# Block two's recurrence: two streams by halves of the tokens, or four streams by quarters with one PSUM bank each

## The reference, cut to what matters

```python
w_log = -softplus(-(w0 + tanh(wd) @ w_lora_up)) - 0.5
decay = exp(-exp(w_log))
a = sigmoid(a0 + ad @ a_lora_up)
g = sigmoid(gd) @ g_lora_up
kk = k * k_k;  kk = kk / max(norm_per_head(kk), 1e-12)
k = k * (1.0 + (a - 1.0) * k_a)
# per token and head, state is 64 x 64:
sa = einsum('bhvk,bhk->bhv', state, -kk_t)
state = state * w_t + sa (x) (kk_t * a_t) + v_t (x) k_t
y = einsum('bhvk,bhk->bhv', state, r_t)
# then: normalised per head, times ln_x_w, plus ln_x_b, plus (sum(r * k * r_k) * v), times g
```

## Time and profile before

| | |
|---|---|
| median of 3 runs | 3462.05 us |
| lowest and highest run | 3459.52 and 3464.85 us |
| profiled execution, first to last instruction | 3458.7 us |
| TensorE busy | 3282.1 us (95%), 24008 matmul rows |
| VectorE, ScalarE, GpSimd busy | 1732.3, 1221.7, 76.4 us |
| chain that ended last | TensorE 79%, VectorE 12%, ScalarE 6% |

### The profile page before, as it was taken

How to read it: one execution, slowest core, us unless ns; L and a number is a source line. 1 busy time by engine, 2 the same in 40 slices (tenths; PEclk the granted TensorE clock), 3 DMA queues, 4 the chain that set the end, 5 groups by cost and what they waited for, 6 DMA issues and landing times.

```text
span 3458.7 us, 55898 instructions
## 1 busy us (share of the span) xinstructions
PE 3282.1 (95%) x24008; PEld 2729.2 (79%) x24008; DVE 1732.3 (50%) x3048; ACT 1221.7 (35%) x2193; POOL 76.4 (2%) x124
## 2 busy tenths in 40 slices
PE   6899999989999999999899998889899999999998
PEld 5788877779888888888777776777677788888887
DVE  8457353345674243346765545454545653433355
ACT  5233454442543221224443222444434431212133
POOL 0000000001000000000000000000000000000000
PEclk9899999999999999999999999999999999999999
DMA  2111122224322111123443122000002231111123
GB/s 103 65 60 62 65 87 77 74 99 131 132 98 86 55 37 55 40 71 130 144 166 127 70 74 84 11 29 29 11 20 98 86 99 54 48 51 47 52 97 110
DMA packets 85238, 262.34 MB, mean 76 GB/s; under 512 B 10208, under 2 KB 10336, under 8 KB 84864
## 3 DMA queue, kind: packets, MB, share of 16 engines
q1 hardware_dynamic: 73056, 217.78, 18.7%
q0 software_dynamic: 7040, 23.16, 1.9%
q10 hardware_dynamic: 4896, 17.84, 1.3%
HBM read 216.51 MB, written 42.21 MB: 75 GB/s over the span
## 4 chain that ended last, share of the span: by engine, by line
PE 79%; DVE 12%; ACT 6%; issue 2%; DMA 1%; DVEq 0%; SPq 0%; ACTq 0%
PE ps L127 76%; PE ps L126 2%; DVE HB L166 2%; PE ps L135 1%; DVE w_lo L166 1%; ACT L145 1%; ACT w_hi L163 1%; DVE HB L176 1%; ACT m_D L145 1%; DVE r_t L166 1%; DVE C L176 0%; DVE r_in L166 0%; DVE m_SS L176 0%; DVE r_Xa L166 0%; DVE a_A L180 0%
## 5 line engine op out<-in xcount | busy, mean ns | idle before, releaser
L166 DVE TENSOR_TENSOR w_lo<-w_raw,w_hi 128x1024 fp32r<-128x1024 f32 (+3 forms) x353 | 393.6, 1115 | 373.1 <-ACT w_hi L163 371.0
L127 PE MATMUL ps<-XHA,w_hi 128*128 128x264 f32 (+3 forms) x1456 | 467.8, 321 | 36.1 <-DVE w_lo L166 31.8
L163 ACT ACTIVATE w_hi<-w_raw 128x1024 fp32r<-128x1024 f32 (+3 forms) x353 | 339.6, 962 | 337.9 <-PE ps L127 281.3
L127 PE MATMUL ps<-XLA,w_hi 128*128 128x264 f32 (+3 forms) x1456 | 458.0, 315 | 0.0
L127 PE MATMUL ps<-XHA,w_lo 128*128 128x264 f32 (+3 forms) x1456 | 456.5, 314 | 0.0
L127 PE MATMUL ps<-XHB,w_hi 128*128 128x512 f32 x920 | 375.5, 408 | 7.0 <-DVE w_lo L166 4.3
L127 PE MATMUL ps<-XLB,w_hi 128*128 128x512 f32 x920 | 360.6, 392 | 0.0
L127 PE MATMUL ps<-XHB,w_lo 128*128 128x512 f32 x920 | 360.5, 392 | 0.0
L127 PEld LDWEIGHTS ps<-XHA,w_hi 128*128 128x128 f32 x1456 | 276.6, 190 | 66.5 <-issue 41.4
L127 PEld LDWEIGHTS ps<-XLA,w_hi 128*128 128x128 f32 x1456 | 276.4, 190 | 21.2 <-issue 3.6
L127 PEld LDWEIGHTS ps<-XHA,w_lo 128*128 128x128 f32 x1456 | 276.9, 190 | 16.4
(11 more groups left out here) (441 smaller groups left out, 6136.0 us busy)
## 6 DMA issues: line engine op xcount, KB each, us to landing
w_raw<-in_f_gate SPq DMA_DIRECT2D x66, 512.0 KB, 3.2
w_raw<-in_f_up SPq DMA_DIRECT2D x66, 512.0 KB, 3.2
w_raw<-in_w_out SPq DMA_DIRECT2D x32, 512.0 KB, 3.3
w_raw<-in_f_down SPq DMA_DIRECT2D x48, 320.0 KB, 2.9
w_raw<-in_f_down SPq DMA_DIRECT2D x32, 384.0 KB, 3.1
w_raw<-in_w_rkv SPq DMA_DIRECT2D x24, 512.0 KB, 3.3
w_raw<-in_w_attn SPq DMA_DIRECT2D x24, 512.0 KB, 3.9
w_raw<-in_w_qkvo SPq DMA_DIRECT2D x16, 512.0 KB, 3.2
```

What stands on the lines that cost most here:

```text
L127: return Issued(e.matmul(out, a, b, start=start, stop=stop))
L163: return Issued(self.eng and self.eng.activation(out, src, ACT.Copy))
L166: return Issued(self.eng and self.eng.tensor_tensor(out, a, b, op))
```

## The change

- Four streams instead of two: stream j has the pair j of heads for all tokens, in four units of 256 tokens (4 chunks). The state stays in five tiles of 64 columns per stream, used in turn, so nothing is kept aside between units. Each stream has one PSUM bank; where two results belong together they share it (`low` and `high` half), and are read in one pass where they are next to each other in SBUF too (`both` is X and Xt).
- Streams start LAG = 9 steps apart. BESIDE is 0.2. The yields of a unit are fewer (36 instead of 55 or 56).
- The decay is applied at the state: S(c+1) = pc * (F^T S(c) + K^T V + B^T U), the last three accumulated in PSUM and scaled by VectorE as it reads them. So e2, e4, `tb2`, `tk2b`, O and its copy are gone; the turns take `be` and `ka` themselves; the shifted decay is read from e1 with an offset of a token.
- Both sigmoids are made as exp(-ln(1 + exp(-x))), with the biases negated once. ScalarE then needs one table set in the recurrence; after the tanh and the sigmoid of the low-rank inputs that set is loaded once.
- The centring of the output is one product with the matrix `centre` (identity less 1/64), the square is taken on ScalarE from PSUM, and scale, bias and bonus are two passes.
- The 67 warming products of the recurrence are gone.
- GpSimd makes `ka` only, and issues the next unit's three loads (256 columns each) once YY is done.

```diff
-LAG, K0, RS, RM, NG, PRE, MID, POST, HN, Q1, Q2, Q3, Q4, Q5 = 20, 1, 3, 5, 4, 42, 18, 8, 8, 1, 1, 1, 1, 1
-
-BESIDE, BEG, ATT = 0.41, 6, 2
+LAG, K0, RS, RM, NG, PRE, MID, POST, HN, Q5 = 9, 1, 3, 5, 4, 42, 18, 8, 8, 1
+
+BESIDE, BEG, ATT = 0.2, 6, 2
...
-    (0, "bon", 1): 3, (0, "bon", 2): 7, (0, "bon", 3): 2, (0, "tA", 2): 2, (0, "tA", 3): 1, (0, ("Y", 0), 0): 10,
...
+STREAMS = (0, 1, 2, 3)
+QUARTERS = (0, 1, 2, 3)
...
+def low(b):
+    return b[:, 0:256]
...
+        self.r, self.k, self.v = D.four[:, 1, :], D.four[:, 2, :], D.four[:, 3, :]
+        self.both = D.four[:, 0:2, :].rearrange("p a x -> p (a x)")
...
+        self.k2, self.e3 = self.a, self.lw
...
+    def state(self, u, c):
+        return self.slots[(4 * u + c) % 5]
...
+        def wide(name, lhs, rhs):
+            b = D.ps.take(P, (name, u))
+            for c in range(4):
+                for h in range(2):
+                    op = P.mm(b[heads(h), 128 * c:128 * c + 128], lhs[heads(h), block(c)],
+                              rhs[heads(h), c, :, :].rearrange("p a x -> p (a x)"), True, True)
...
+        b = D.ps.take(P, ("la", u))
+        P.mm(low(b), K.wl[0:32, 128 * j:128 * j + 128], tokens(K, u, slice(0, 32)), True, True).then_inc(S.pe)
...
+        P.mm(high(b), K.wl[32:64, 128 * j:128 * j + 128], tokens(K, u, slice(32, 64)), True, True).then_inc(S.pe, ("la", u))
+        yield
+        dense64("n2", low(D.ps.take(P, ("n2", u))), K.ones64, x.bn, S.dve, ("kk2", u))
...
+        b = D.ps.take(P, ("tVA", u))
...
+        turn("tV", low(b), lambda c: x.v[:, block(c)])
...
+        turn("tA", high(b), lambda c: x.AR[:, c, 0, :])
+        yield
+        b = D.ps.take(P, ("tBK", u))
+        P.wait_ge(S.dve, ("tbe", u))
...
+        turn("tK", high(b), lambda c: x.ka[:, block(c)])
...
+        wide("GB", x.be, x.AR)
+        yield
+        wide("GK", x.ka, x.AR)
...
+            b = D.ps.take(P, (("Y", lv), u))
...
+            products(("Y", lv), b, lambda h, c: [(x.GB[heads(h), c, 0, :], x.X[heads(h), block(c)])])
...
+            b = D.ps.take(P, ("Xt", u, lv))
...
+                products(("X", lv), low(b), lambda h, c: [(x.Xt[heads(h), block(c)], x.Y[heads(h), block(c)])])
+            products(("Xt", lv), high(b), lambda h, c: [(x.Y[heads(h), block(c)], x.Xt[heads(h), block(c)])])
...
+        wide("WU", x.Xt, x.AM)
...
+        for c in range(4):
+            if u < 3 or c < 3:
...
+                    P.mm(b[heads(h), 0:64], x.Kt[heads(h), block(c)], x.Vt[heads(h), block(c)], True, False)
+                    op = P.mm(b[heads(h), 0:64], x.Bt[heads(h), block(c)], x.WU[heads(h), c, 1, :], False, first)
+                if not first:
+                    P.wait_ge(S.dve, ("F", u))
+                    P.wait_ge(S.dve, ("S", 4 * u + c))
+                    for h in range(2):
+                        op = P.mm(b[heads(h), 0:64], x.FT[heads(h), block(c)], x.state(u, c)[heads(h), :], False, True)
+                op.then_inc(S.pe, ("S", u, c))
...
+        b = D.ps.take(P, ("out", u))
+        dense64("cen", low(b), K.centre[:, :], x.yy, S.act, ("YY", u))
+        yield
+        dense64("var", high(b), K.ones64, x.sq, S.act, ("sq", u))
+        yield from pause(2)
...
+        P.mm(high(b), K.gl[0:96, 128 * j:128 * j + 128], tokens(K, u, slice(0, 96)), True, True).then_inc(S.pe, ("g", u))
...
+        A.act(x.lw, low(ps["la", u]), ACT.Exp, bias=K.vec("w0", j), scale=-1.0).then_inc(a)
+        A.act(x.a, high(ps["la", u]), ACT.Exp, bias=K.vec("a0", j), scale=-1.0).then_inc(a, ("la", u))
...
+        A.act(x.la, x.la, ACT.Ln).then_inc(a)
...
+        A.act(x.la, x.la, ACT.Exp, scale=-1.0).then_inc(a, ("sig", u))
...
+        A.act(x.AR[:, :, 1, :], by64(x.cum), ACT.Exp, scale=-DECAY).then_inc(a, ("e1", u))
+        A.act(x.e3, x.cum, ACT.Exp, scale=DECAY).then_inc(a, ("e3", u))
+        A.act(x.pc, by64(x.cum)[:, :, 63], ACT.Exp, scale=-DECAY).then_inc(a, ("pc", u))
...
+        kept("tK", "tBK", x.kc, ps["tBK", u][:, :])
...
+        A.act(x.sq, low(ps["out", u]), ACT.Square).then_inc(a, ("sq", u))
...
+        V.ts(x.la, x.la, 1.0, 1e35, ADD, MIN).then_inc(d, ("la1", u))
...
+        V.vcopy(x.AR[:, :, 0, 0:1], by64(x.kk)[:, :, 0:1]).then_inc(d)
+        V.tt(x.AR[:, :, 0, 1:64], x.AR[:, :, 1, 0:63], by64(x.kk)[:, :, 1:64], MUL).then_inc(d, ("tal", u))
...
+        V.tt(x.AR[:, :, 1, :], x.AR[:, :, 1, :], by64(x.r), MUL).then_inc(d, ("trho", u))
...
+        V.tt(x.be, x.bn, x.e3, MUL).then_inc(d, ("tbe", u))
...
+            V.tt(out.rearrange("p c a x -> p c (a x)"), ps[name, u][:, :].rearrange("p (c x) -> p c x", x=128),
+                 K.mtri[:, :].unsqueeze(1).broadcast_to([128, 4, 128]), MUL).then_inc(d, (name, u))
...
+        V.tt(by64(x.both), by64(x.both), repeat(K.ident2[:, :], 8), ADD).then_inc(d, ("Xt", u, 0))
...
+            V.tt(by64(x.Y), by64(low(ps[("Y", lv), u])), level(2 + lv), MUL).then_inc(d, ("Y", u, lv))
...
+                V.tt(x.both, x.both, ps["Xt", u, lv][:, :], ADD).then_inc(d, ("Xt", u, lv + 1))
+            else:
+                V.tt(x.Xt, x.Xt, high(ps["Xt", u, lv]), ADD).then_inc(d, ("Xt", u, lv + 1))
...
+        V.tt(by64(x.FT), by64(low(ps["F", u])), repeat(K.ident2[:, :], 4), ADD).then_inc(d, ("F", u))
...
+                V.ts(x.state(u, c + 1)[:, :], ps["S", u, c][:, 0:64], x.pc[:, c:c + 1], None, MUL).then_inc(
+                    d, ("S", 4 * u + c + 1))
...
+        V.stt(x.yy, low(ps["out", u]), K.vec("ln_w", j), x.rs, MUL, MUL).then_inc(d, ("cen", u))
...
+        V.stt(x.yy, x.yy, K.vec("ln_b", j), x.bon, ADD, ADD).then_inc(d)
...
+        for other in STREAMS:
+            if other != j and j in (0, 3):
+                V.wait_ge(K.rws[other].pe, ("g" if j else "la", u))
+        V.tt(K.HB[:, j, 256 * u:256 * u + 256], x.yy, high(ps["g", u]), MUL).then_inc(d, ("y", u))
...
+        G.wait_ge(S.dve, ("k2", u))
+        G.tt(x.ka, x.k2, x.e3, MUL).then_inc(S.pool, ("tka", u))
+        yield from pause(27)
+        if u < 3:
+            G.wait_ge(S.pe, ("YY", u))
+            rwkv_load(G, K, j, u + 1)
+        yield from pause(4)
...
+    begin, step = {s: LAG * n for n, s in enumerate(streams)}, 0
     while streams:
+        for s in list(streams):
+            if step >= begin.get(s, 0) and next(s, END) == END:
+                streams.remove(s)
...
+    L.streams = [rwkv(L, K, j) for j in STREAMS]
...
-    K.rw = [Kernel(), Kernel()]
-    for g in range(2):
-        K.rw[g].ps, K.rw[g].ld = Banks(ps[2 * g:2 * g + 2]), K.named(f"rw{g}_in")
+    K.rw = [Kernel() for _ in STREAMS]
+    for j, D in enumerate(K.rw):
+        D.ps, D.ld = Banks(ps[j:j + 1]), K.named(f"rw{j}_in")
```

More of the change, by code:

```diff
@@ L2175, in in3_act @@
             A.act(w, w, ACT.Sigmoid).then_inc(S.act, ("gd", c))
+            A.table(LN_EXP)
 def in3_dve(V, K):
@@ new lines, in rwkv_pe @@
+        P.wait_ge(S.dve, ("tbe", u))
+        turn("tB", low(b), lambda c: x.be[:, block(c)])
+        P.wait_ge(S.pool, ("tka", u))
+        turn("tK", high(b), lambda c: x.ka[:, block(c)])
[3 more added lines that the diff above has]
+        wide("GK", x.ka, x.AR)
+        yield
+        products("L", D.ps.take(P, ("L", u)), lambda h, c: [(x.AR[heads(h), c, 0, :], x.be[heads(h), block(c)])])
+        yield
+        b = D.ps.take(P, ("MV", u))
+        P.wait_ge(S.act, ("tV", u))
@@ new lines, in rwkv_pe @@
+        products("F", b, lambda h, c: [(x.WU[heads(h), c, 0, :], x.Bt[heads(h), block(c)])])
+        yield
+        products("R", D.ps.take(P, ("R", u)), lambda h, c: [(x.WU[heads(h), c, 0, :], x.GB[heads(h), c, 1, :])])
+        yield
+        for c in range(4):
+            if u < 3 or c < 3:
+                b, first = D.ps.take(P, ("S", u, c)), u == 0 and c == 0
+                for h in range(2):
+                    P.mm(b[heads(h), 0:64], x.Kt[heads(h), block(c)], x.Vt[heads(h), block(c)], True, False)
[6 more added lines that the diff above has]
+                op.then_inc(S.pe, ("S", u, c))
+            yield
@@ L2467, in rwkv_act, with kept @@
+        yield
+        dense64("var", high(b), K.ones64, x.sq, S.act, ("sq", u))
+        yield from pause(2)
+        b = D.ps.take(P, ("g", u))
+        P.wait_ge(K.in3.act, ("gd", u // 2))
+        P.mm(high(b), K.gl[0:96, 128 * j:128 * j + 128], tokens(K, u, slice(0, 96)), True, True).then_inc(S.pe, ("g", u))
+        S.pe.at["end", u] = S.pe.n
+        yield
+def rwkv_act(A, K, j):
+    D, S = K.rw[j], K.rws[j]
+    x = Quarter(D)
+    a, ps = S.act, D.ps
     yield from pause(BEG)
     first_half_over(A, K)
-    for u, (j, hf) in enumerate(halves(g)):
-        half_over(A, S, u, a)
-        for name, out, vec in (("lw", x.lw, "w0"), ("a", x.a, "a0")):
+    A.wait_ge(K.c.dve, "bias")
+    for u in QUARTERS:
+        def kept(name, group, out, src):
@@ L2539, in rwkv_act, with rwkv_dve @@
[L2539 to L2555 removed]
+def rwkv_dve(V, K, j):
+    D, S = K.rw[j], K.rws[j]
+    x = Quarter(D)
@@ L2724, in rwkv_load, with rwkv_pool @@
-def rwkv_load(D, K, g, u):
-    T, (j, hf) = K.rw[g], halves(g)[u]
```

(20 more changed lines are left out.)

532 lines of the change are left out of this document (162 added, 370 removed), and 2 rows, old and new, of the table WARM.

## The result

The changed kernel takes 3411.73 us, the median of 4 runs (3405.33 to 3418.99), against 3462.3 us before (3459.52 to 3464.85). The ratio is 0.9855, with a 95% interval of 0.9843 to 0.9868: 50.6 us less, where the prediction said 76 us less and a range of 3333 to 3450 us. The direction and the range held; the gain is two thirds of what was forecast. Of the ten executions of one later kernel, the one with 80 warming products, two took 6549 and 15471 us and are left out of its median.

What follows compares the result with a forecast made beforehand. TensorE, busy for 95% of the span, was taken as the bound, so time had to come from its work or waits. Stretches of 214 + 435 + 50 = 699 us against 775 gave 3386 us, range 3333 to 3450 us.

Steps and rivals of the forecast that it cites:

- the band of 50 to 105 us: Whole kernel: the forecast gain around 76 us less, given a chance of 0.60.
- TensorE's work and the waits for the chains: Block two's recurrence: TensorE's work falls by 32 us, idle time beside the attention to 0.15 us a step.
- First stretch: Second half's 26 dense tiles projected beside the recurrence: 286 us become 214 us, 72 us less, mostly moved.
- Middle: Recurrence beside the attention, 136 steps at 2.70 + 0.50 us: 435 us, bounds 394 and 466 us.
- The tail: Attention alone after the last stream ends, 26 steps: 50 us, bounds 47 and 68 us.
- the moved work is not absorbed: Rival: idle time stays at 0.73 us a step, tail at lower clock, 3446 us; gains of 7 to 50 us: 0.16.
- The sum: Whole stage: 214 + 435 + 50 = 699 us against 775, 76 us less, giving 3386 us.
- What was costed at nothing: VectorE at 2.1 and ScalarE at 1.5 us a step, below 2.70; TensorE's 32 us less work not counted directly.
- One bank closes the ring: Slower rival: a stream's next group waits until its bank is read; 4.25 us a step, 3529 us; chance 0.11.
- All idle time goes: Rival, whole stage: 3333 us, more than 105 us off; chance 0.10.
- No difference: Rival: the chains are hidden already, so the change doesn't do what it says; chance 0.03.

Runs made afterwards that it cites:

- the clock held: 25 extra products of 256 columns (10.7 us) ahead of first turns in the last pair of heads' block rows 3 to 7, against the changed kernel: 3400.2 us.
- doubled passes: Each of the 80 VectorE passes that read Y run twice, same result, against the changed kernel: 3417.9 us.

## Why the prediction was right, and where it was off

The gain of 50.6 us lies at the very edge of the band of 50 to 105 us that had 0.60; the repeat of the change, 3407.7 us, lies 4 us inside it. That the band held is in part luck, since one term of the sum failed.

**TensorE's work and the waits for the chains.** Right. The forecast was that four streams cover each other's chain, and the waits for the inverse would be under 10 us: they are 2.0 us. TensorE's idle time in the middle is 0.21 us a step (28.8 us over 136 steps), where 0.15 was forecast and 0.37 stood before.

**First stretch, 214 us forecast, 207 measured.** The term was right in kind. The rest of 0.29 us a step was too much: 207 less 156 and 46 us of work leaves 0.12 us a step. TensorE has 0.3 us of idle time in it. Most of these 79 us are moved, as forecast, and the kernel with BESIDE 0.1 shows that the middle takes moved work at 3.3 us a step over all, work included.

**Middle, 435 us forecast, 444 measured.** 444 less 367 us of work are 0.57 us a step where 0.50 was forecast. The 0.36 us that I "let stand" for changes of shape and clock stood (0.57 less 0.21 of idle time), but not by its parts: the clock's was at most 0.12 us a step before (half of 41 us over 164 steps) and is at most 0.03 now (half of 7 us over 136), so the other part, by the prediction the changes of shape, must have grown. What was off is the idle time, 0.21 for 0.15 us a step, and its largest part is the state (11.1 us), whose chain I had not priced for its four steps a unit with a pass of 282 ns.

**The tail, 50 us forecast, 65 us measured: the term that failed.** The step is the sentence "Alone, a pair goes scores, two exponentials, copies, values, scores: 1.0 + 2 x 1.35 + 1.2 + 1.8 + 1.6 us and hand-overs, 8.9 us for 1024 columns". Its durations were taken from rows at full clock, from a place where the recurrence stood between. Alone, TensorE waits in each pair, the granted clock falls to 1.2 GHz, and a pair of 896 columns takes 14.5 us. The bound of 68 us was in the text, under the rival "the moved work is not absorbed", and its clock condition came true in this stretch alone. The prediction calls itself wrong if the end is over 68 us with a low clock there: the first profile has 65.3 us, the repeat 71.5, so this sign was met in one of two profiles. With the clock held, the end is 55.6 us with 10.7 us of added work in it, of which part stands in waits. So the forecast of 50 us would have been near for a chain at full clock; no run shows that without added products.

**The sum.** 207 + 444 + 65 = 716 us against 699: 17 us of the 26 us that are missing. Another 4 us lie ahead of the stage in the profiled run, and the timed median is 6 us above that run.

**What was costed at nothing.** VectorE: the prediction's slope and the fixed part gave 0.42 us for 256 columns, measured 0.422, and the stage has 380.8 us of VectorE, 53% and not the 56% of the forecast; that 34 us of doubled passes cost 5 to 10 us shows that it is nearly covered, not fully. The Trainium skill ("VectorE: DVE Perf Modes", section "The TRN2 errata") gives an fp32 `tensor_tensor` of N columns (N + 151) cycles at 0.96 GHz, 0.157 us of them fixed. The trace agrees: 422 ns for 256 columns and 685 ns for 512, where the formula has 424 and 691. The same section advises tiles of 512 elements or more. The change goes against that, and yet VectorE is busy for 380.8 us in the stage instead of 392.8, since steps were taken out. ScalarE: 97 table loads as forecast, but "nothing" was wrong for what they were worth: the kernel with table sigmoids is 11 to 15 us slower, so the exponentials in place of the sigmoid table bring up to a quarter of the gain. The warming products: the prediction says that it counts nothing for their removal, but its sum holds it, since it sets 338 us of the recurrence's work against 306. In the two-stream kernel the removal would have cost 15 us. They aren't needed with four streams, where 80 of them make the stage 57 us longer. So of the 55 us between the profiled runs some 30 us are products that the four streams made needless, and 25 us are idle time.

**The rivals.** *One bank closes the ring:* out, by the waits and by the doubled passes. The Trainium skill ("Perfetto Trace Analysis", Matmuls) asks that independent groups rotate through banks. Here one stream has one bank, but successive groups on TensorE belong to different streams and so to different banks, and the reading of one stands beside the products of the next: with that the rule is kept, and the trace's 2.0 us of waits agree. *All idle time goes:* out, 28.8 us stay in the middle. *Not absorbed:* true of the end only. *No difference:* out, by the interval of the ratio.

**Left open.** How much four streams bring by themselves, and how much the decay at the state and the smaller number of passes, was not taken apart; that the waits for the inverse went is measured, that the number of streams alone did it is argued. What moving alone is worth, with two streams, has no run that gives a time. Nor is it known why the clock of the middle is better now: fewer gaps are the likely reason, as the two-stream kernel without warming products has more gaps and a lower clock, but the two were not separated.
